# Moving the exp of a choice's gates to a later slot of a gather-bound expert layer

## The reference, cut to what matters

```python
s_top, i_top = lax.top_k(s, 16)                         # 2 x 128 scores per token and head
cand = s_top[:, :, 0, :, None] + s_top[:, :, 1, None, :]   # 256 candidates
best, pos = lax.top_k(cand.reshape(T, 8, 256), 16)
gates = jax.nn.softmax(best, axis=-1)
...
act = jax.nn.gelu(jnp.einsum('cd,ced->ce', xb, u[eb]), approximate=False) * gb
y   = jnp.einsum('ce,ced->cd', act, v[eb])
```

## Time and profile before

| | us |
|---|---|
| median of 3 runs (1835.69 to 1846.94) | 1836.91 |
| the profiled execution, its own time | 1839.5 |
| its span in the trace | 1837.7 |
| TensorE busy | 1614.7 (88%) |
| VectorE busy | 1208.4 (66%) |
| ScalarE busy | 829.3 (45%) |
| GpSimd busy | 373.6 (20%) |

### The profile page before, as it was taken

How to read it: one execution, slowest core, us unless ns; L and a number is a source line. 1 busy time by engine, 2 the same in 40 slices (tenths; PEclk the granted TensorE clock), 3 DMA queues, 4 the chain that set the end, 5 groups by cost and what they waited for, 6 DMA issues and landing times.

```text
span 1837.7 us, 24081 instructions
## 1 busy us (share of the span) xinstructions
PE 1614.7 (88%) x9325; PEld 1219.7 (66%) x9325; DVE 1208.4 (66%) x2403; ACT 829.3 (45%) x1701; POOL 373.6 (20%) x327
## 2 busy tenths in 40 slices
PE   7878998699878767888888988989999999999999
PEld 6768997555423323322242878879999875579999
DVE  5577566778787888454655767546775547567764
ACT  5555544444544444333533643235554425346542
POOL 1010012345444443434442003100000100010000
PEclk9889999899988888999999989989999999899999
DMA  6322452799999999999998221114445421025544
GB/s 255 119 88 93 161 183 94 318 387 427 425 414 394 401 392 397 415 427 427 427 427 355 98 86 48 69 69 161 165 165 164 172 92 69 1 93 184 185 170 149
DMA packets 63593, 421.15 MB, mean 229 GB/s; under 512 B 8180, under 2 KB 11512, under 8 KB 15608
## 3 DMA queue, kind: packets, MB, share of 16 engines
q0 software_dynamic: 36864, 268.45, 35.4%
q1 hardware_dynamic: 23952, 148.70, 22.5%
q10 hardware_dynamic: 2664, 2.47, 0.4%
HBM read 418.54 MB, written 1.05 MB: 228 GB/s over the span
## 4 chain that ended last, share of the span: by engine, by line
PE 63%; DMA 16%; DVE 12%; ACT 7%; issue 2%; POOL 0%; SPq 0%; ACTq 0%; DVEq 0%
PE bank L306 61%; DMA uv<-in_uv,idx 16%; DVE lows L369 2%; DVE uv L1355 2%; ACT L318 1%; PE bank L2525 1%; ACT acts L318 1%; ACT dg L318 1%; DVE cacc L322 1%; PE bank L311 1%; ACT wf L314 1%; ACT wp L314 1%; DVE t L322 0%; DMA xT<-in_xT 0%; DVE nq L2564 0%
## 5 line engine op out<-in xcount | busy, mean ns | idle before, releaser
L306 PE MATMUL bank<-uv,dg 128*128 128x512 f32 x1024 | 497.2, 631 | 119.1 <-ACT dg L318 117.4
L306 PEld LDWEIGHTS bank<-uv,dg 128*128 128x128 f32 x1024 | 193.7, 199 | 412.3 <-ACT dg L318 212.9
L1355 DVE CUSTOM_DVE_ANT_0 uv<-uv,htok 128x1024 f32<-128x1024 f32 x256 | 313.2, 1224 | 183.8 <-DMA uv<-in_uv,idx 182.3
L1469 POOL DMA_INDIRECT uv<-in_uv,idx x256 | 294.2, 1149 | 381.7 <-PE bank L306 325.1
L369 DVE TENSOR_TENSOR lows<-slabs,wp 128x2048 fp32r<-128x2048 f32 (+1 forms) x78 | 167.7, 2151 | 50.7 <-ACT wp L314 50.5
L306 PE MATMUL bank<-hn,lows 128*128 128x272 f32 (+2 forms) x704 | 200.9, 285 | 0.0
L484 POOL TENSOR_TENSOR sqT<-sqT 128x256 f32<-128x256 f32 (+1 forms) x42 | 46.2, 1100 | 690.2 <-ACT sqT L318 687.9
L314 ACT ACTIVATE wp<-slabs 128x2048 fp32r<-128x2048 f32 (+1 forms) x78 | 140.6, 1803 | 84.4 <-DMA slabs<-in_dn 27.2
L318 ACT ACTIVATE acts<-acts 128x1 f32<-128x1 f32 x256 | 50.3, 197 | 195.7 <-DVE acts L1355 195.3
L306 PE MATMUL bank<-hh,lows 128*128 128x272 f32 x448 | 135.1, 302 | 0.0
L306 PEld LDWEIGHTS bank<-hn,lows 128*128 128x128 f32 x704 | 132.6, 188 | 0.0
(11 more groups left out here) (383 smaller groups left out, 3027.3 us busy)
## 6 DMA issues: line engine op xcount, KB each, us to landing
slabs<-in_up SPq DMA_DIRECT2D x44, 1024.0 KB, 4.8
slabs<-in_w_in SPq DMA_DIRECT2D x28, 1024.0 KB, 4.9
slabs<-in_dn SPq DMA_DIRECT2D x32, 704.0 KB, 4.0
slabs<-in_wkv SPq DMA_DIRECT2D x8, 1024.0 KB, 4.8
slabs<-in_w_out SPq DMA_DIRECT2D x8, 1024.0 KB, 4.8
slabs<-in_pq SPq DMA_DIRECT2D x8, 1024.0 KB, 4.8
slabs<-in_wq SPq DMA_DIRECT2D x4, 1024.0 KB, 4.9
slabs<-in_wo SPq DMA_DIRECT2D x4, 1024.0 KB, 4.8
```

Source lines behind the costliest of these rows:

```text
L306: ins = T.e.matmul(pr[2] if len(pr) > 2 else out, pr[0], pr[1], start=(start and k == 0), stop=(stop and k == len(pairs) - 1), skip_group_ ...
L1355: V.e.tensor_tensor_reduce(u_, u_, htok[:, n, :], 1.0, 0.0, ALU.mult, ALU.add, acts[:, n, e_:e_ + 1]).then_inc(*V.up("dot", q))
L1469: G.e.indirect_dma_start(uv[q % NU][:, :], None, d["uv"][:, :], bass.IndirectOffsetOnAxis(ap=idx[:, n, e_:e_ + 1], axis=0)).then_inc(s_uv[ ...
```

## The change

The exp becomes an item of its own, `("gexp", n, h)`, that only ScalarE reads. For the first choice it stands where it stood. For each other choice, made in slot q, it is put behind `("v", q)`, which is in slot q + 2; if step 18 of the choice comes before that, it is put just ahead of step 18. By the list this is never needed: all 15 stand behind `("v", q)`. For the other engines the order of the list is the same as before.

```diff
-            out = first + second[:7] + [("tokens",)] + second[7:] + scores_of(1)
+            out = first + second[:7] + [("tokens",)] + second[7:11] + [("gexp", 0, 0)] + second[11:] + scores_of(1)
...
-            taken = {("choose", 0, 0, 18)}
+            taken, late = {("choose", 0, 0, 18)}, []
-            def pump(steps):
+            def pump(steps, q):
                 for x in todo[:steps]:
+                    if x[0] == "choose" and x[3] == 18 and late:
+                        out.append(late.pop()[1])
                     out.append(x)
                     taken.add(x)
+                    if x[0] == "choose" and x[3] == 10:
+                        late.append((q, ("gexp",) + x[1:3]))
                 del todo[:steps]
...
                 if q >= LAG:
                     out.append(("v", q - LAG))
+                    if late and late[0][0] <= q - LAG:
+                        out.append(late.pop()[1])
...
-                elif x[0] == "choose" and x[3] == 10:
-                    _, n, h, _ = x
+                elif x[0] == "gexp":
+                    _, n, h = x
                     g = gat[:, n, h, :]
                     A.wait_ge(*V.at("ch", n, h, "gap"))
```

More of the change, by code:

```diff
@@ L1240, in peer_plan @@
                     while ("choose", n, e_ // 16, 18) not in taken:
-                        pump(1)
+                        pump(1, q)
                     out.append(("u", q))
-                    pump(3 if q < 16 else 2)
+                    pump(3 if q < 16 else 2, q)
                     if q >= EARLY and (q - EARLY) % 3 == 0 and q < EARLY + 30:
```

## The result

The changed kernel takes 1822.47 us (median of 6 runs, 1821.1 to 1828.57) against 1838.64 us for the kernel before in the same comparison. The ratio is 0.9902, with a 95% interval from 0.9881 to 0.9923: 18.0 us less by the ratio (14.2 to 21.9). The forecast was 17.0 us, 0.93%. The profiled execution takes 1821.1 us with a span of 1819.3.

The account below looks back on a forecast made before the run. It took DMA gathers of `uv`, with a 427 GB/s ceiling, to bound the stretch from 333 to 1005 us. Gains of 15.5 and 1.9 less 0.4 made -17.0 us: 1836.9 to 1819.9 us, range 1815 to 1830.

Parts of the forecast that it names:

- the 9 waits: 505 to 750 us: ScalarE's 55.5 us of waiting for the difference that step 10 writes would fall to near 0.
- The sum: Whole kernel: 15.5 us from 505 to 760 us plus 1.9 early, less 0.4 for new holds, 17.0 us gained.
- The term of the late exps: 505 to 760 us: rate back from 400 to 427 GB/s, 16.1 us less 0.6 for its start and slot 129.
- the term of the early ones: 340 to 505 us: 1.9 us gained at head 1's exp, less 0.4 for small new holds.
- The hold: ScalarE at each exp: load, exp, load take 2.90 us, making the next row 1.45 us late instead of 7.2.
- The path may be 8.8 us late once: Gather path: 8 buffers x 2.45 = 19.6 us against 10.8 needed, so 8.8 us of lateness before DMA runs dry.
- ring: The 8 row buffers the gathers fill in turn, said to take 8.8 us of lateness once.
- The lateness of 8.9 us: GpSimd at a choice in the kernel before: issues 11.4 us after its last gather where 2.45 is the pace.
- The 6.1 us made good between two exps: Over the 9.5 rows between exps TensorE catches up 6.1 us, leaving about 2.8 us lost per exp.
- the 16.1 read from the rate: 505 to 760 us: time missing at 400 against 427 GB/s; preferred to 22 us worked out over 8 exps.
- the lower clock: TensorE at 1.2 GHz after idling 7.62 us, given the rest of the lateness beyond ScalarE's 7.2 us.
- The longest gap between gathers: 505 to 750 us: longest gap between GpSimd's gather issues under 5 us instead of 11.

Follow-up runs that it names:

- behind_two: Changed kernel with the exp just behind the row it stood ahead of, so ScalarE waits for 2 rows; 0.9928 of the kernel before.
- hold_two: Changed kernel with one more Exp and Gelu pair of table loads ahead of each of the nine late exps; 1827.0 against 1845.4 us, one run each.
- before_warm: Kernel before with 6 extra, unread fp32 products on TensorE at each of the nine late exps; 0.9928 of the kernel before.

## Why the prediction was right

**Direction, place and mechanism** were right. The rate from 505 to 760 us is the 427 GB/s foreseen, the 9 waits are gone, the last dot product starts at 989.6 us (988 foreseen), and no wait of VectorE for the exp appears. At head 2, the tightest place, the exp starts at 383.12 and the reciprocal at 385.91: VectorE has 2.5 us of room from the end of the exp, against "up to 3".

**The sizes.** The sum was 17.0 us. The gather stretch gave 14.3 and 13.9 us in the two profiles of the changed kernel. The term of the late exps was 15.5 us and measured 13.0 alone; the term of the early ones was 1.9 less 0.4 and measured 2.5 alone. The late term was too large by 2.5 us. Counted by rows, the change saves 1.4 us up to row 57 and 14.0 from there to row 160, and then 1.1 us of it are lost again behind row 160, where the sum had nothing; why is not shown. From the dot of row 57 to that of row 150 it took 245.5 us and now takes 231.4, against 93 x 2.45 = 227.9 at the pace of a gather: 3.5 us stay, some at slot 129 and at the gaps told of at the end. That the timed gain is 18.0 us, above the sum, is no merit of it: its interval starts at 14.2.

**The hold.** Said to be 2.90 us, with the next row 1.45 us late; measured 2.92 us, and the row 1.45 us behind its turn (526.73 against a turn of 2.45 us behind the Gelu at 522.83). Whether the clock falls for a pause of under 2 us was left open. It does at the first late exp (0.74 for 6 us) and at none of the seven others with a pause of 1.91 us.

**Two steps of the reasoning failed,** though the number didn't rest on them. First, the room and the lateness were both too large. "The path may be 8.8 us late once": out of a nearly full ring, `behind_two` is 6.3 us late in the mean and already loses a little at each exp, while `hold_two`, 6.0 us late, loses next to nothing. So about 6 us are free, not 8.8. The lateness of 8.9 us was read from one exp, the one of the nine with the most; their mean is 7.5. The 6.1 us made good between two exps are right (6.2 by the leads). With the measured sizes the account gives 8 x (7.3 - 6.2) = 9 us for the eight later exps, where 14.0 us were lost over all nine. The dot products slip before the lead is down to 6 us (that of row 81 comes 5.25 us behind row 80's, with a lead of 8.5); how the remaining 5 us come about is not shown. That the working gave 22 us, near the 16.1 read from the rate, made it look sounder than it was. Secondly, the lower clock was put down as "the rest" of the lateness, 1.7 of 8.9 us. As most of the lateness is free and only what exceeds the room is paid, the clock weighs far more than its share: `before_warm` gets 8.5 us back, against 14.3 for the change, with waits only 0.6 us shorter. Its ring is also fuller ahead of the eight later exps, with a lead of 14.0 us in the mean instead of 13.0.

**A miss in the signs.** The longest gap between gathers was to be under 5 us. It is 8.3 us, from 677.73 to 686.01:

```profile
677.73 0.94 POOL L1477 DMA_INDIRECT uv<-in_uv,idx  x1 [1.26 <-PE bank L306]
686.01 0.95 POOL L1477 DMA_INDIRECT uv<-in_uv,idx  x1 [7.35 <-PE bank L306]
```

TensorE waits there for VectorE to take out block 0's accumulators:

```profile
681.10 1.25 PE L311 MATMUL bank<-con,sqT 128*128 128x128 f32 x8 [3.65 <-DVE sqT L1375]
```

This is slot 129, which the sum had charged with a part of 0.6 us. The ring takes it: 429 GB/s from 681 to 687 us, and at least 419 in the two windows of 6 us behind.

## What to carry to other kernels

When engines share one order, an instruction that waits for another engine belongs behind the work that it doesn't need; two slots further on the list were worth 1% of the whole kernel, without an instruction less. Price such a wait by what it exceeds: find how late the path may be before the bound resource (here the DMA engines) runs dry, and whether that room is back before the next wait. Look at that resource in short slices rather than by its mean, and expect a curve, 20, 10, 3 and 1 us for equal steps. Near the edge of that room, a small cause such as a lower clock behind a pause can carry more than half of the loss, and most of the gain is had before the wait is wholly gone.

## What the runs showed of the hardware that was not expected

The dot products of the changed kernel come 2.45 us apart but for a few places, such as 3.43 us ahead of row 92. There VectorE waits 1.06 us for the gather, while the DMA engines still move 423 GB/s. The same 3.43 us stand ahead of row 92 in `behind_two` and `before_warm`, so it belongs to the program and not to chance.

In those 5 us (582 to 587) the queues show, besides the gathers, one packet of instructions. It is tempting to blame it. From 505 to 975 us the trace of the changed kernel holds 22 such packets. Five of them start 1.9 to 2.6 us ahead of a dot product that comes 2.85 to 3.43 us behind the last one (rows 73, 92, 113, 167 and 219), and so does the packet ahead of row 92 in `behind_two`. But the others come without such a gap. One of them lies between 562 and 567 us with the dot products 2.45 us apart on both sides, and three start 2.2 us ahead of rows 123, 184 and 243, which are on time; the gaps ahead of rows 207, 210 and 228 come without a packet. So a packet is not enough to make a row late, and what does is open.
